# A float32 transformer block and two recurrent and attention layers on one Trainium2 core: eight modulation pieces move from TensorE to GpSimd

## What is computed

```python
mod = (c_act @ w_ada[l] + b_ada[l])[:, None, :]          # first block: 6 x 1024 columns
mod = jax.nn.silu(c) @ w + b                             # second block: four of 3 x 1024 columns
# delta rule, of each head and chunk: a unit lower triangular system of 64 rows
sol = jax.lax.linalg.triangular_solve(t_mat, rhs, left_side=True, lower=True, unit_diagonal=True)
```

## Time and profile before

| | |
|---|---|
| median of three runs | 2995.43 us (2989.66 to 2995.61) |
| the profiled execution | 2987.68 us, span 2986.0 us |
| mean granted TensorE clock | 0.961 |
| PE / DVE / ACT / POOL busy | 92% / 38% / 16% / 8% |
| last pieces by TensorE and the inverse | 258.6 to 361.2 us |
| the scan | 361.2 to 404.7 us |
| the window's attention | 404.7 to 448 us |

### The profile page before, as it was taken

One profiled execution on the slowest core, in us unless ns is written; L12 is line 12 of the kernel. 1 busy time (PEld: TensorE's weight loads), 2 busy tenths in 40 slices (PEclk: granted clock), 3 DMA queues, 4 the chain that ended last, 5 costly groups with the idle time before them and its releaser, 6 DMA issues.

```text
span 2986.0 us, 37205 instructions
## 1 busy us (share of the span) xinstructions
PE 2748.3 (92%) x15695; PEld 1353.8 (45%) x15695; DVE 1139.2 (38%) x1423; ACT 465.3 (16%) x916; POOL 238.3 (8%) x364
## 2 busy tenths in 40 slices
PE   7988989698899989999995999999999999999998
PEld 3446765232223322232332465477554334546763
DVE  3865453411111111121123254454536663344544
ACT  1122042000000000000000143000013662200001
POOL 1000011011111001101011500000000110000000
PEclk9988989799999999999997999999999999999999
DMA  9776411889999999999999112132223223221310
GB/s 338 282 254 231 179 30 48 315 344 407 401 381 397 409 406 407 409 406 400 413 409 367 38 59 90 57 113 79 90 59 71 58 64 113 106 85 57 112 57 28
DMA packets 170833, 639.49 MB, mean 214 GB/s; under 512 B 75907, under 2 KB 77531, under 8 KB 138129
## 3 DMA queue, kind: packets, MB, share of 16 engines
q1 hardware_dynamic: 156818, 607.76, 53.2%
q0 software_dynamic: 13792, 29.39, 3.4%
q10 hardware_dynamic: 64, 0.07, 0.0%
HBM read 626.44 MB, written 15.23 MB: 215 GB/s over the span
## 4 chain that ended last, share of the span: by engine, by line
PE 50%; issue 33%; DMA 5%; DVE 5%; POOL 3%; POOLq 2%; ACT 2%; DVEq 1%; SPq 0%; ACTq 0%
PE ps L2442 10%; PE ps L2477 10%; PE ps L2780 4%; PE ps L2513 4%; PE ps L2157 3%; DMA slots<-in_ada_w_dram 2%; PE ps L3036 2%; PE ps L2407 2%; PE ps L2324 2%; PE ps L2427 2%; PE ps L1221 2%; POOLq L1677 2%; DMA slots<-in_w_ada_dram 2%; PE ps L2796 1%; POOL work L1686 1%
## 5 line engine op out<-in xcount | busy, mean ns | idle before, releaser
L1787 PE MATMUL ps<-slots,hT 128*32 128x512 f32 x5120 | 564.6, 599 | 13.5 <-DMA slots<-in_w_up_dram 12.4
L1787 PEld LDWEIGHTS ps<-slots,hT 128*32 128x32 f32 x5120 | 165.6, 111 | 387.7 <-issue 365.0
L2477 PE MATMUL ps<-slots,work 128*128 128x512 f32 x672 | 289.6, 592 | 2.8 <-DVE work L2555 2.8
L1825 PE MATMUL ps<-slots,work 128*32 128x512 f32 x2112 | 247.8, 613 | 48.0 <-DMA slots<-in_w_down_dram 46.1
L1939 DVE TENSOR_SCALAR stage<-ps 128x512 f32<-128x512 f32 (+1 forms) x47 | 32.2, 686 | 548.8 <-PE ps L1791 548.4
L2477 PEld LDWEIGHTS ps<-slots,work 128*128 128x128 f32 x672 | 127.5, 190 | 162.5 <-issue 157.8
L2442 PE MATMUL ps<-hT,slots 128*128 128x256 f32 x768 | 168.7, 379 | 0.0
L1825 PEld LDWEIGHTS ps<-slots,work 128*32 128x32 f32 x2112 | 69.9, 112 | 196.3 <-issue 191.0
L2780 PE MATMUL ps<-hT,slots 128*128 128x512 f32 x352 | 156.6, 601 | 0.0
L2442 PEld LDWEIGHTS ps<-hT,slots 128*128 128x128 f32 x768 | 145.9, 190 | 22.4 <-issue 2.9
L2652 DVE TENSOR_TENSOR work<-work,ps 128x1024 f32<-128x1024 f32 x60 | 71.6, 1218 | 165.2 <-PE ps L2477 164.9
(11 more groups left out here) (587 smaller groups left out, 3431.2 us busy)
## 6 DMA issues: line engine op xcount, KB each, us to landing
slots<-in_w_up_dram SPq DMA_DIRECT2D x128, 2048.0 KB, 20.3
slots<-in_w_down_dram SPq DMA_DIRECT2D x64, 2048.0 KB
slots<-in_mlp_w_dram SPq DMA_DIRECT2D x32, 2048.0 KB, 7.9
slots<-in_ada_w_dram SPq DMA_DIRECT2D x40, 1024.0 KB, 4.9
slots<-in_w_ada_dram SPq DMA_DIRECT2D x16, 1024.0 KB, 5.6
slots<-in_w_in_dram SPq DMA_DIRECT2D x5, 2048.0 KB, 15.7
slots<-in_rnn_w_in_dram SPq DMA_DIRECT2D x24, 384.0 KB, 4.2
slots<-in_w_ada_dram SPq DMA_DIRECT2D x4, 2048.0 KB, 12.6
```

The costliest lines, as they stand in the source:

```text
L1787: ins = pe.matmul(to, x[:, k, unit * UNIT:(unit + 1) * UNIT], upw[s][:, k % 2, col:col + CH], start=k == 0, stop=False)
L1825: ins = pe.matmul(to, actT[:, 4 * q + j, 64 * u + 32 * h:64 * u + 32 * h + 32], downw[sl[h]][:, j, half * CH:(half + 1) * CH], start=k == ...
L2477: ins = pe.matmul(ps[:, bank + t], x[:, k, t * P:(t + 1) * P], w[:, k], start=k == 0, stop=k == HK - 1)
```

## The change

Pieces 24 to 31 (g = 6 and 7) leave TensorE's loop. They are loaded as 16 units of 128 rows by 2048 columns (1 MB), alternately into the two halves of slot 4; a unit's load waits until the unit two before it is done. GpSimd scales each unit by its column of c in two instructions of 128x1024, and adds it to a sum in slot 5 in four of 128x512, with a drain behind each kind; the first unit of a group is scaled straight into the sum. TensorE does the two sums over the partitions (`side_pe`), the first in the scan's chunk n = 1, the second behind the scan; ScalarE's copies and stores of g = 6 and 7 move with them. Pieces 20 and 21 stay before step 0; 22 and 23 move one step later, to steps 1 and 2. Group 5 and group 6 change columns, and their bias loads are cut in other places (eight instead of six). The load of `swb` moves from GpSimd's queue to SP's; the second half of w_out's load waits for the last modulation. ScalarE no longer waits at the stage's end for the stores to land: GpSimd does so behind the meeting.

```diff
@@ ada_slot, ada_pieces @@
+        POOL_FIRST = 6
+        POOL_UNITS = (N_ADA - POOL_FIRST) * KT
+        ADA_SLOT = (4, 5, 4, 5)
+        POOL_BEFORE = 1 + 2 * ADA_SLOT.count(4)
-            return SIDE_SLOT if n < N_SIDE else 4 + (n - N_SIDE) % 2
+            return SIDE_SLOT if n < N_SIDE else ADA_SLOT[n - N_SIDE]
...
-            if g < 6:
-                return [(w2v[g - 2], 0, 4 * CH, A2 + (g - 2) * 3 * D)]
-            return [(w2v[l], 4 * CH, HALF, A2 + l * 3 * D + 4 * CH) for l in (2 * (g - 6), 2 * (g - 6) + 1)]
+            if g < 5 or g == 6:
+                l = 3 if g == 6 else g - 2
+                return [(w2v[l], 0, 4 * CH, A2 + l * 3 * D)]
+            return [(w2v[l], 4 * CH, HALF, A2 + l * 3 * D + 4 * CH) for l in ((2, 3) if g == 5 else (0, 1))]
@@ ada_bias_loads: three loads for each half become four @@
+                g.dma_start(dst[2:5], b2v[0:3, half * D:(half + 1) * D]).then_inc(S("dnw_in"), 16)
...
@@ ada_sp @@
-            for n in range(N_SIDE, 4 * N_ADA):
+            for n in range(N_SIDE, 4 * POOL_FIRST):
...
+            for h in range(POOL_UNITS):
+                g, k = POOL_FIRST + h // KT, h % KT
+                if h < 2:
+                    sp.wait_ge(freed[4], loads[4])
+                else:
+                    sp.wait_ge(S("side_free"), N_SIDE + h - 1)
+                dst, src = ada_slots[:, 4, h % 2], w2v[3, k * P:(k + 1) * P, 0:4 * CH]
+                if g == 7:
+                    dst, src = dst.rearrange("p (l n) -> p l n", l=2), w2v[0:2, k * P:(k + 1) * P, 4 * CH:4 * CH + HALF].rearrange("l p n -> p l n")
+                sp.dma_start(dst, src).then_inc((landed[4], S("side_in"))[h % 2], 16)
+
+        def pool_part(h):
+            return ada_slots[:, 4, h % 2].rearrange("p (j n) -> p j n", j=4)
+
+        def pool_sum(pool, g):
+            acc = side_acc(g)
+            for k in range(KT):
+                h = (g - POOL_FIRST) * KT + k
+                if h == 0:
+                    pool.wait_ge(freed[5], 2 + ADA_SLOT.count(5))
+                if h % 2 == 0:
+                    pool.wait_ge(landed[4], 16 * (POOL_BEFORE + h // 2 + 1))
+                else:
+                    pool.wait_ge(S("side_in"), 16 * (N_SIDE + h // 2 + 1))
+                part = pool_part(h)
+                for j in (slice(0, 2), slice(2, 4)):
+                    ins = pool.tensor_scalar((part if k else acc)[:, j], part[:, j], cT[:, 1, k:k + 1], None, ALU.mult)
+                pool.drain()
+                if k:
+                    for j in range(4):
+                        ins = pool.tensor_tensor(acc[:, j], acc[:, j], part[:, j], ALU.add)
+                ins.then_inc(S("side_free"), 1)
+                pool.drain()
@@ side_acc @@
-            return slots[:, g - 3, KT // 2:KT]
+            if g < POOL_FIRST:
+                return slots[:, g - 3, KT // 2:KT]
+            return slots[:, 5, 0:KT // 2] if g == POOL_FIRST else slots[:, 5, KT // 2:KT]
@@ side_pe @@
-            pe.wait_ge(S("side_free"), 4 * (g + 1))
+            if g < POOL_FIRST:
+                pe.wait_ge(S("side_free"), 4 * (g + 1))
+            else:
+                pe.wait_ge(S("side_free"), N_SIDE + KT * (g - POOL_FIRST + 1))
@@ dn_moves @@
-            sp.dma_start(swb, A["k_swbias"].rearrange("p (h n) -> p h n", h=SH)).then_inc(S("dnw_in"), 16)
+            sp.dma_start(swb, A["k_swbias"].rearrange("p (h n) -> p h n", h=SH)).then_inc(S("proj_in"), 16)
@@ dn_pe, in the loop of the inverse @@
                 if i == 10:
                     pe.wait_ge(S("sw_made"), 1)
+                    pe.wait_ge(S("v_out"), TT)
...
-                if N_SIDE + 2 + i < 4 * N_ADA:
-                    ada_pe(pe, N_SIDE + 2 + i)
+                if i in (1, 2):
+                    ada_pe(pe, N_SIDE + 1 + i)
@@ dn_pe, in and behind the loop of the scan @@
                 ins.then_inc(S("ws_ps"), 1)
+                if n == 1:
+                    side_pe(pe, POOL_FIRST)
...
+            side_pe(pe, POOL_FIRST + 1)
+            assert uses[4] == POOL_BEFORE
+            uses[4] += POOL_UNITS // 2
@@ dn_act @@
-            for g in range(N_SIDE // 4, N_ADA):
-                ada_act(a, g)
+            ada_act(a, N_SIDE // 4)
...
                 a.copy(vn[u % 2][r], ps[r, u % 2].rearrange("p (h d) -> p h d", h=DH)).then_inc(S("v_new"), 1)
+                if n == 1:
+                    ada_act(a, POOL_FIRST)
...
-            a.wait_ge(S("ada_out0"), 64 * 4)
-            a.wait_ge(S("ada_out1"), 64 * 4)
+            ada_act(a, POOL_FIRST + 1)
@@ sw_dve @@
-            v.wait_ge(S("dnw_in"), 192)
+            v.wait_ge(S("proj_in"), 96 + 16)
@@ block.sync @@
-                pair_sp(sp, A["w_out"][0], 4)
+                dn_moves(sp)
+                sp.wait_ge(S("side_free"), N_SIDE + POOL_UNITS)
+                load(sp, 4, wview(A["w_out"][0, :, 0:CH]))
+                sp.wait_ge(S("ada_done"), N_ADA + 1)
+                load(sp, 5, wview(A["w_out"][0, :, CH:2 * CH]))
@@ block.gpsimd @@
-                dn_moves(g); end()
+                pool_sum(g, POOL_FIRST)
+                pool_sum(g, POOL_FIRST + 1); end()
+                for p in range(2):
+                    g.wait_ge(S(f"ada_out{p}"), 64 * N_ADA // 2)
                 second_mods(g); mod_turned_loads(g)
```

More of the change, by code:

```diff
@@ L320, in ada_bias_loads @@
                 g.dma_start(dst[0:2], A["b_ada"][0, 2 * D:6 * D].rearrange("(g h n) -> g h n", g=2, h=2)[:, half]).then_inc(S("dnw_in"), 16)
-                g.dma_start(dst[2:6], b2v[:, half * D:(half + 1) * D]).then_inc(S("dnw_in"), 16)
-                g.dma_start(dst[6:8], b2v[:, 2 * D:3 * D].rearrange("(g h) n -> g h n", h=2)[:, half]).then_inc(S("dnw_in"), 16)
+                g.dma_start(dst[2:5], b2v[0:3, half * D:(half + 1) * D]).then_inc(S("dnw_in"), 16)
+                g.dma_start(dst[5:6], b2v[2 + half:3 + half, 2 * D:3 * D]).then_inc(S("dnw_in"), 16)
+                g.dma_start(dst[6:7], b2v[3:4, half * D:(half + 1) * D]).then_inc(S("dnw_in"), 16)
+                g.dma_start(dst[7:8], b2v[half:half + 1, 2 * D:3 * D]).then_inc(S("dnw_in"), 16)
         def side_src(n, kk):
@@ L391, in side_pe @@
                 pe.wait_ge(S("c_silu"), 1)
-                pe.wait_ge(S("dnw_in"), 80 + 96)
+                pe.wait_ge(S("dnw_in"), 80 + 160)
             if g >= 2:
                 pe.wait_ge(S("ada_read"), g)
-            pe.wait_ge(S("side_free"), 4 * (g + 1))
+            if g < POOL_FIRST:
+                pe.wait_ge(S("side_free"), 4 * (g + 1))
+            else:
+                pe.wait_ge(S("side_free"), N_SIDE + KT * (g - POOL_FIRST + 1))
             for j in range(4):
@@ L1003, in dn_dve @@
                     if i == TT:
-                        v.wait_ge(S("dnw_in"), 176)
+                        v.wait_ge(S("dnw_in"), 240)
                     m = mixed[:, i - TT, 0:CH].rearrange("p (h d) -> p h d", h=DH)
```

## The result

| | before | after |
|---|---|---|
| median of the runs compared (4 each) | 2992.55 us | 3036.08 us |
| lowest to highest | 2984.17 to 2995.61 us | 3033.21 to 3039.3 us |
| ratio after / before, 95% interval | | 1.015 [1.0125, 1.0175] |
| profiled execution, its span | 2987.68, 2986.0 us | 3039.3, 3037.7 us |
| mean granted clock | 0.961 | 0.946 |

The change makes the kernel 1.5% slower, 43.5 us between the medians. Forecast were 2982 us, a gain of 13.5; the result lies outside the range, on the other side.

What follows compares the result with a forecast made beforehand. TensorE and 2 MB weight transfers were taken to pace the inverse's steps with a piece. Gain 19.9 - 4.0 (hold-ups) - 2.4 (scan) = 13.5 us, from 2995.43 to 2982; range 2976 to 2995.

Steps and rivals of the forecast that it cites:

- GpSimd's own chain: Sixteen units scaled and added on GpSimd, scalings and additions at 1.0 us each: 104.8 us from 277.5, done at 382.3.
- The two paces of the inverse, and 19.9 us up to step 12: Inverse: 5.5 us a step with a piece, 3.5 without; step 12 reached at 313.2 instead of 333.06 us.
- Hold-ups of 4 us: VectorE's instructions reading two SBUF tensors wait for GpSimd: 0.8 us in steps 4 to 7, 3.2 in `sw_scales`.
- the 8.5 us that were left as a risk: Steps 3 to 19: gain lost if each of 17 VectorE corrections, taken as free, were held up by half an addition.
- The sums over the partitions: Scan: the first sum costs 2.0 us and small operations 0.4; the second fits behind TensorE's end.
- the rival without hold-ups: VectorE isn't delayed by GpSimd at all: gain 17.5 us, 2978; chance 0.07.
- An addition of 1.0 us: GpSimd's additions of 128x512 follow one another at 1.0 us, from 2.04 for two.
- The cover of 4.9 us: End of stage: GpSimd's second group must be done at 386.3 against 391.2; each 0.1 us more of a scaling uses 3.2.
- Edits at no cost: Two more bias loads, the moved `swb` load and the later w_out loads delay nothing.
- the slower one: GpSimd's scaling takes 2.04 us, TensorE waits behind the scan, stage ends 14.9 us later: 3010; chance 0.08.
- The clock: Inverse: less TensorE work drops the clock to 1.2 GHz, 14 us slower; chance 0.04. Sign of error: PEclk under 0.95, 280 to 340 us.
- GpSimd is the last, a little: A scaling takes 1.49 us, GpSimd done at 398.0, stage end 402: gain 2.7 us, 2992.7; chance 0.17 with the corrections' hold-up.

Runs made afterwards that it cites:

- Experiment 4: Changed kernel with the scalings moved to ScalarE, one activation of 128x2048 a unit, GpSimd only adding in instructions of 128x512: 2978.85 us, ratio 0.996 to the kernel before.
- additions only: Changed kernel with GpSimd's scalings left out except the first unit's of each group: 2985.37 us, ratio 0.996 to the kernel before.
- GpSimd idle: Changed kernel with all of GpSimd's arithmetic left out, waits and signals kept: 2973.25 us, ratio 0.9929 to the kernel before.

## Why the prediction was wrong

**The step that failed** is in GpSimd's own chain: no row showed a scaling, it was bounded by a memset (0.94) and two additions (2.04), and 1.0 was taken because "one read of twice the columns costs as much as the addition". It measured 2.83 us alone and 2.89 in the kernel, beyond the upper bound. Both bounds reasoned from how many operands are read; what decides is which operation is done, and that none of the rows showed. The Trainium skill (GPSIMD Engine Reference, "Engine selection") has GpSimd roughly at line rate with one input; that holds here for the copy (1.0 us) and not for the scaling. Its advice to keep such work off GpSimd was right for the scalings; the additions, which the same row would keep off it too, paid once ScalarE did the scalings (Experiment 4).

**The sum again, with what was measured.** GpSimd worked from 274.40 to 442.95, 168.6 us, against 104.8 forecast: 60.1 more for the scalings (92.1 - 32), 14.9 more for the additions (70.9 - 56), 0.7 more between the instructions, and 12.0 less, since the waits for a load (2.5) and for VectorE (9.5) that were added are inside the measured means or not there. It began 3.1 us earlier. 60.1 + 14.9 + 0.7 - 12.0 - 3.1 = 60.6, and 382.3 + 60.6 = 442.9. Behind it 6.1 us to the attention instead of 4: the sum runs at half clock. So 449.0, and 449.07 is measured. The stage is 47.2 us longer, and the attention, at a lower clock, 3.0 us (49.4 against 46.5). Between the medians lie 43.5 us; the interval of the ratio, 37 to 52 us, covers both.

Point by point:
- *The two paces of the inverse, and 19.9 us up to step 12:* right. 21.0 us, counted from step 0. Pieces 22 and 23 in steps 1 and 2 fit as worked out: step 4 stood at 278.76, 18.9 us behind step 0, where 19.5 was forecast.
- *Hold-ups of 4 us:* right in size, between the 2.8 us of after and the 6.2 beside additions only, and in part right in place: the end of `sw_scales` (L1039 of after) costs, while L1060 cost nothing in after, where TensorE's wait stayed 0.58 in steps 5 to 8. Half of the 2.8 is no hold-up of VectorE's but the half clock behind TensorE's longer wait, a term that the forecast didn't have. Corrections and masks aren't held up, 0.68 to 0.69 us in every kernel, so the 8.5 us that were left as a risk are excluded.
- *The sums over the partitions:* the scan and what follows take 45.7 us with additions only (350.5 to 396.2) against 43.6 before, 2.1 more, where 2.4 were forecast.
- *The gain of 13.5 of the stage, had GpSimd been fast enough:* 12.3 with additions only, 11.5 with ScalarE's scalings; 18.5 with GpSimd idle, where 17.5 was given for the rival without hold-ups.
- *An addition of 1.0 us:* wrong, 1.23 alone and 1.30 here, from a row of squares, whose two inputs are one tensor. Its 14.9 us are about what the separate terms for hold-ups and the load, 12.0, gave back.
- *The cover of 4.9 us:* the forecast called it thin and gave the price of a miss, 3.2 us for each 0.1 us of a scaling. A scaling was 1.83 us dearer, and that is the whole loss.
- *Edits at no cost:* bias loads, `swb` and w_out weren't waited for. The scores' wait stands at ScalarE's drain, 2.18 us, not at a transfer.
- *The rivals:* the slower one had the right mechanism, its place and its mark (TensorE waits behind the scan), but a price of 2.04 us, and so 3010 in place of 3036. The clock fell in the inverse, but only behind the wait of step 14; from 280 to 340 us it has a mean of 0.97, above the 0.95 that was to be the mark, and the steps without a wait kept 3.49 us. The rival "GpSimd is the last, a little" didn't come about.
- *Chances:* the turn to a loss, 1.6 us a scaling, stood inside the forecast's own bounds, 0.94 to 2.04, with 4 tenths of them beyond it. With a price that no row shows, multiplied by 32 on a cover of 4.9 us, 0.08 for that side was far too little.

**What stays open:** why a scaling takes GpSimd 2.7 times as long as a copy. The runs exclude the column (2.74 with a constant), contention (2.83 alone) and a fixed cost; what within the operation takes the time they don't show. That VectorE is held for only 1.0 of its 2.8 us speaks for time spent away from what the two engines share, but that is argued, not shown. It is also open whether additions placed clear of `sw_scales` would bring the last 7 us.

## What to carry to other kernels

Before work is moved to another engine, have a row of exactly that operation on that engine: the price of its neighbours (a memset, a square, a copy) bounds nothing. If no row exists, take the number at which the change turns to a loss and ask how sure it is that the price is below it. And in a split between engines give each part to the one that is fast at it: here ScalarE scaled 2048 columns in 2.00 us, GpSimd only added, in short instructions, and the change became 0.4% faster instead of 1.5% slower.

## What the runs showed of the hardware

- GpSimd, float32, 128 partitions, from start to start: scaling 1024 columns 2.83 us (column) or 2.74 (constant), 512 columns 1.55; copy of 1024 1.0; 512 columns of an addition or product of two different tensors 1.23, of one tensor with itself or with a spread column 1.01; an addition of 2048 columns 4.52.
- A multiplication by a column is faster as a product with that column spread over the row (2.02 us for 1024 columns) than as a scaling (2.83).
- GpSimd's additions held VectorE's instructions on SBUF up to their whole length, some with one input too (3.55 us for 128x8). Its scalings of 2.84 us held those with two inputs for their first 1.0 us only (0.82 us for an instruction 0.84 us in, 0.69 for one 2.45 us in, 1.45 for one 0.54 us in), and once a copy to their end. With an input in PSUM VectorE never was held up.
- After the waits of 7.67 and 47.09 us TensorE was found at half its clock (0.50), and its next 8 products of 128x512 took 1.9 us instead of the 1.06 of the earlier trace rows. Behind the wait of 3.27 us in the inverse of after it fell to 0.50 for some 3 us as well; behind the waits of 1.68 us (before, and without GpSimd's work) it stayed 1.00.
